# Two layer norms whose normalised copy is left out: x is turned and split block by block, and the row scale is applied at the eviction

## The chip, the cores and the metric

The kernel runs on one core of a Trainium2 chip. The metric is the device time of one execution in microseconds (us). Runs of one kernel mostly agree within 0.3%.

## The reference

Three layers over 256 tokens of width 2048, all in float32. The change touches the way into the first two, "ab" and "c". Both begin in the same way:

```python
def _rmsnorm(x, g):
    x32 = x.astype(jnp.float32)
    y = x32 * lax.rsqrt(jnp.mean(x32 * x32, axis=-1, keepdims=True) + NORM_EPS)
    return y * g.astype(jnp.float32)

h = jnp.matmul(_rmsnorm(x, norm_g).astype(x.dtype), w_in)      # 256 x 2048 by 2048 x 8192
# ab: 8 heads of a dilated mixture and 4 heads of differential attention, c: 16 heads of causal attention
x = x + jnp.matmul(y.astype(x.dtype), w_out)                   # 256 x 2048 by 2048 x 2048
```

The third layer (an ada-modulated mixer and a sparse expert layer) keeps its code.

## The kernel before

The tokens lie in two blocks of 128 partitions (T = 2). A GEMM is done in tiles of 512 output columns. Each tile is 16 steps (K = 16), one for each block of 128 rows of the weight. At each step ScalarE (ACT) rounds a 128x512 piece of the weight to `w_hi` (`split_hi_act`, L501, its instruction on L507), VectorE (DVE) writes the rest `w_lo` (`split_lo_dve`, L509), and TensorE (PE) runs six matmuls of 512 columns (`multiply_pe`, L514: hi by hi, hi by lo, lo by hi, for both token blocks). `w_hi` and `w_lo` are rings of four, so ACT can be at most four steps ahead of PE. SyncE (SP) streams the weight in pieces of two steps, 512 KB each, into `raw`, a ring of four pieces.

The other operand is x, normalised, turned (tokens along the free axis) and split in the same way into `xt_hi` and `xt_lo`. This was done in a stage of its own ahead of each of the two layers: `normalise_act` and `normalise_dve` (L425 to L432) take the mean square of each row, its root and a Newton step, and write the normalised copy `xn`. `turn_pe` (L434) then turns 32 blocks of 128x128 in eight groups, ACT and DVE apply the norm's weight g to them (L468, L488), and ACT and DVE split them (L473, L479). `end_of_stage` (L304) is a barrier of PE, ACT and DVE: each drains and waits for the other two. There is one behind the turning and one behind layer ab.

Inside a layer (`layer_act`, `layer_pe`, `layer_dve`, L615 to L702) the order of all work is written out by the step number s: 256 steps of the way in (16 tiles), then 64 steps of the way out (4 tiles). The attention of each pair of heads is placed at fixed steps between (`pairs_pe`, `pairs_act`, `pairs_dve`). `take_tile_act` (L635) evicts a tile of the way in from PSUM into `h` four steps into the next tile, `take_residual` (L706) adds a tile of the way out to x. GpSimd (POOL) streams 96 pieces of 1 MB of the ada weight into a ring of two (`ada_pool`, L528), and DVE adds each to an accumulator (`modulate`, L553) at the steps in ADA_SLOTS. The sum of such a piece over the partitions is `sum_cols_pe` (L970), at steps 38 and 42 of the way out.

At the start SP issues the load of x as one transfer, then sixteen constants, and then the weight (L2136 to L2146). PE's first instruction waits for all constants (L1849).

## Time and profile before

| | us |
|---|---|
| median of three runs | 3513.04 (3511.92 to 3519.26) |
| the profiled execution's own time | 3512.95 |
| its span in the trace | 3511.2 |

| engine | busy us | share |
|---|---|---|
| PE, matmuls | 3114.0 | 89% |
| DVE | 2489.3 | 71% |
| ACT | 1880.1 | 54% |
| POOL | 314.5 | 9% |

The span is the distance from the first to the last instruction in the trace; the rest of the execution's time, 1.75 us, lies around it. Times of single instructions below are from the span's start. A matmul's listed duration holds its way through the array, so that the pace is read from the distance between two starts. The granted clock is TensorE's, as a share of 2.4 GHz.

### The profile page before, as it was taken

The page shows a single profiled execution, that of the slowest core. Times are in us where ns is not written, and L with a number is a line of the kernel's source. Part 1 is how long each engine was busy: PE and PEld are TensorE (multiplying, and loading weights), DVE is VectorE, ACT ScalarE, POOL GpSimd, SP SyncE. Part 2 cuts the span into 40 slices and gives each one's busy share as a digit, 9 for nine tenths or more (in the row PEclk, how much of TensorE's full clock was granted, in tenths as well). Part 3 has the DMA queues.
Part 4 walks back from the last instruction along what each step waited for, and adds up shares of the span by engine and source line. Part 5 has one row for each costly group of instructions (what it writes and reads, how often), then busy time and mean ns, then how long its engine had stood idle before and what let it go on. Part 6 is the DMA issues. An engine that isn't in the chain of part 4 may idle for free. (4 is left out here: it accounts for less than half of the span.)

```text
span 3511.2 us, 45806 instructions
## 1 busy us (share of the span) xinstructions
PE 3114.0 (89%) x12426; PEld 2181.8 (62%) x12426; DVE 2489.3 (71%) x4415; ACT 1880.1 (54%) x4088; POOL 314.5 (9%) x422
## 2 busy tenths in 40 slices
PE   5999987999995959995795759999999899999997
PEld 4887766888884847884574612222222488888885
DVE  5778766777766857864655889998888655555555
ACT  4555544555544444544344447777777655555553
POOL 0000000000000000000000023333333100000000
PEclk9999998999997969996896955555555699999998
DMA  5666654666674907970053269999999755555553
GB/s 191 215 207 215 196 196 158 228 222 208 222 244 139 364 0 284 347 254 30 13 180 110 97 250 387 379 354 381 389 382 375 303 190 191 191 191 190 191 190 128
DMA packets 213960, 788.27 MB, mean 225 GB/s; under 512 B 18514, under 2 KB 19666, under 8 KB 151250
## 3 DMA queue, kind: packets, MB, share of 16 engines
q1 hardware_dynamic: 159904, 407.33, 34.1%
q0 software_dynamic: 50688, 369.12, 27.9%
q10 hardware_dynamic: 3252, 10.41, 0.8%
q8 instruction: 56, 0.92, 0.1%
q14 instruction: 60, 0.49, 0.0%
HBM read 781.55 MB, written 5.24 MB: 224 GB/s over the span
## 5 line engine op out<-in xcount | busy, mean ns | idle before, releaser
L511 DVE TENSOR_TENSOR w_lo<-raw,w_hi 128x512 fp32r<-128x512 f32 x880 | 584.8, 693 | 308.1 <-ACT w_hi L507 248.7
L507 ACT ACTIVATE w_hi<-raw 128x512 fp32r<-128x512 f32 x640 | 399.7, 631 | 497.4 <-PE bank L522 489.9
L1749 DVE CUSTOM_DVE_ANT_0 u_ring<-u_ring,bank 128x1024 f32<-128x1024 f32 x512 | 604.2, 1217 | 78.7 <-DMA u_ring<-in_peer_u,idx 54.7
L1816 DVE TENSOR_TENSOR w_lo<-v_raw,w_hi 128x512 fp32r<-128x512 f32 x512 | 354.1, 692 | 300.1 <-ACT w_hi L1800 300.1
L1661 PE MATMUL bank<-row_ring,three 3*128 3x512 bf16 x1024 | 511.1, 616 | 40.3 <-DVE act_in L1749 24.7
L1800 ACT ACTIVATE w_hi<-v_raw 128x512 fp32r<-128x512 f32 x512 | 323.5, 632 | 332.8 <-PE bank L1838 328.6
L520 PE MATMUL bank<-w_hi,xt_hi 128*128 128x512 f32 x1024 | 409.4, 400 | 19.9 <-DVE w_lo L511 19.9
L1836 PE MATMUL bank<-w_hi,vw_hi 128*128 128x512 f32 x1024 | 398.7, 389 | 7.2 <-DVE w_lo L1816 7.2
L1838 PE MATMUL bank<-w_hi,vw_lo 128*128 128x512 f32 x1024 | 404.4, 395 | 0.0
L1837 PE MATMUL bank<-w_lo,vw_hi 128*128 128x512 f32 x1024 | 402.5, 393 | 0.0
L522 PE MATMUL bank<-w_hi,xt_lo 128*128 128x512 f32 x1024 | 400.7, 391 | 0.0
L521 PE MATMUL bank<-w_lo,xt_hi 128*128 128x512 f32 x1024 | 400.5, 391 | 0.0
L558 DVE SCALAR_TENSOR_TENSOR acc<-ada_ring,c_col,acc 128x2048 f32<-128x2048 f32 x128 | 301.0, 2351 | 12.2 <-issue 0.4
L353 ACT ACTIVATE w_hi<-raw 128x512 fp32r<-128x512 f32 x304 | 190.3, 632 | 219.3 <-PE bank L372 188.4
L1632 POOL DMA_INDIRECT u_ring<-in_peer_u,idx x256 | 246.3, 962 | 456.2 <-DVE act_half L1749 452.9
L1661 PEld LDWEIGHTS bank<-row_ring,three 3*128 3x128 bf16 x1024 | 67.1, 106 | 316.8 <-DVE act_half L1749 223.0
L1669 PEld LDWEIGHTS bank<-hot_side,hot_side 128*128 128x128 f32 x512 | 128.1, 311 | 214.7 <-ACT hot_side L1712 208.0
L370 PE MATMUL bank<-w_hi,xt_hi 128*128 128x512 f32 x608 | 240.4, 395 | 18.2 <-DVE w_lo L511 15.0
L371 PE MATMUL bank<-w_lo,xt_hi 128*128 128x512 f32 x608 | 239.3, 394 | 0.0
L372 PE MATMUL bank<-w_hi,xt_lo 128*128 128x512 f32 x608 | 239.0, 393 | 0.0
L520 PEld LDWEIGHTS bank<-w_hi,xt_hi 128*128 128x128 f32 x1024 | 193.6, 189 | 61.0 <-issue 17.1
L1836 PEld LDWEIGHTS bank<-w_hi,vw_hi 128*128 128x128 f32 x1024 | 192.9, 188 | 50.6 <-issue 7.4
(336 smaller groups left out, 4564.1 us busy)
## 6 DMA issues: line engine op xcount, KB each, us to landing
v_raw<-in_peer_v SPq DMA_DIRECT2D x128, 1024.0 KB, 4.8
ada_ring<-in_ada_w POOLq DMA_DIRECT2D x96, 1024.0 KB, 5.6
raw<-in_w_in_ab SPq DMA_DIRECT2D x128, 512.0 KB, 3.9
raw<-in_w_in_c SPq DMA_DIRECT2D x128, 512.0 KB, 4.1
raw<-in_w_in SPq DMA_DIRECT2D x120, 512.0 KB, 6.0
raw<-in_w_out_ab SPq DMA_DIRECT2D x32, 512.0 KB, 4.5
raw<-in_w_out_c SPq DMA_DIRECT2D x32, 512.0 KB, 5.0
raw<-in_w_out SPq DMA_DIRECT2D x32, 512.0 KB, 4.4
```

Of the source, the lines that this page charges most:

```text
L507: act.activation(w_hi[:, s % WS, :], raw[:, q % RAW, s % KC, :], ACT.Copy).then_inc(hi_ready, 1)
L511: dve.tensor_tensor(w_lo[:, s % WS, :], raw[:, s // KC % RAW, s % KC, :], w_hi[:, s % WS, :].bitcast(F32), ALU.subtract).then_inc(raw_used, 1)
L520: pe.matmul(o, a_hi, b_hi, start=kk == 0, stop=False, skip_group_check=True)
L521: pe.matmul(o, a_hi, b_lo, start=False, stop=False, skip_group_check=True)
L522: last = pe.matmul(o, a_lo, b_hi, start=False, stop=kk == K - 1, skip_group_check=True)
L1661: last = pe.matmul(bank[:, 2 * hf + b, :], three[k:k + 3, :], rows_slot(j)[:, c:c + 512], start=True, stop=True)
L1749: dve.tensor_tensor_reduce(u, u, bank[:, 2 * hf:2 * hf + 2, :].rearrange("p b n -> p (b n)"), 1.0, 0.0, ALU.mult, ALU.add, (act_in, act_ha ...
L1800: act.activation(w_hi[:, c, :], v_raw[j][:, c * N:(c + 1) * N], ACT.Copy).then_inc(values_high, 1)
L1816: dve.tensor_tensor(w_lo[:, c, :], v_raw[j][:, c * N:(c + 1) * N], w_hi[:, c, :].bitcast(F32), ALU.subtract).then_inc(values_split, 1)
L1836: pe.matmul(o, a_hi, w_hi[:, c, :], start=first and j == 0, stop=False, skip_group_check=True)
L1837: pe.matmul(o, a_hi, w_lo[:, c, :], start=False, stop=False, skip_group_check=True)
L1838: last = pe.matmul(o, a_lo, w_hi[:, c, :], start=False, stop=True, skip_group_check=True)
```

## The change

- The normalised copy goes, with both normalise stages, both turning stages and the four barriers around them. x itself is turned, scaled by g and split, in eight pieces of two blocks (`x_turn_pe`, `x_high_act`, `x_low_dve`). The mean square's root r is applied to the rows of the tiles of the way in, as the scale operand of their eviction.
- Layer ab turns pieces 0 and 1 ahead of step 0 and pieces 2 to 7 at steps 0, 2, ... 10. PE waits ahead of each even step under 16 for `xt_lo` of that piece. Layer c has pieces 0 to 5 turned inside ab's way out (steps 38, 42, 46, 50, 55, 59) and pieces 6 and 7 at its own steps 6 and 8.
- The row sums of squares are taken at step 6 (ACT) and 7 (DVE) in ab, both on ACT at step 6 in c; the root and its Newton step at steps 10, 13 and 15.
- x is loaded in four pieces of 512 KB, each ahead of one piece of the weight on SP. eye and g of ab go to ACT's queue. Thirteen constants and c_col go to POOL's, behind x. ada's first two pieces come behind c_col.
- The accumulators are not cleared; the first addition writes. The first two slots of `modulate` in ab move from steps 4 and 18 to 20 and 23. The last residual tile of ab is added at step 3 of c. The lambda of ab moves by 14 to 22 steps.

```diff
+        LATE = (38, 42, 46, 50, 55, 59)
+        def x_turn_pe(pe, v, i):
+            if v:
+                pe.wait_ge(evacuated, PRE + plan["ab_out"]["t0"] + i // 2 + 1)
+            else:
+                pe.wait_ge(x_landed[i // 2], 16)
+            if i >= 2:
+                pe.wait_ge(lo_written, PRE + NG * v + i - 1)
+            for j in range(2):
+                for t in range(T):
+                    last = pe.transpose(bank[:, 4 + i % 2, (j * T + t) * P:(j * T + t + 1) * P],
+                                        x[:, t, (2 * i + j) * P:(2 * i + j + 1) * P], eye[:, :])
+            last.then_inc(blocks_turned, 1)
+        def x_high_act(act, v, i):
+            act.wait_ge(blocks_turned, PRE + NG * v + i + 1)
+            for j in range(2):
+                k = 2 * i + j
+                last = act.activation(xt_hi[:, k, :], bank[:, 4 + i % 2, j * S:(j + 1) * S], ACT.Copy, scale=(g_ab, g_c)[v][:, k:k + 1])
+            last.then_inc(hi_written, 1)
+        def x_low_dve(dve, v, i):
+            dve.wait_ge(hi_written, PRE + NG * v + i + 1)
+            for j in range(2):
+                k = 2 * i + j
+                last = dve.scalar_tensor_tensor(xt_lo[:, k, :], bank[:, 4 + i % 2, j * S:(j + 1) * S], (g_ab, g_c)[v][:, k:k + 1],
+                                                xt_hi[:, k, :].bitcast(F32), ALU.mult, ALU.subtract)
+            last.then_inc(lo_written, 1)
+        def layer_norm_pe(pe, v, s):
+            if v == 0 and s == 0:
+                pe.wait_ge(eye_landed, 32)
+                x_turn_pe(pe, 0, 0)
+                x_turn_pe(pe, 0, 1)
+            if v == 0 and s % 2 == 0 and s <= 10:
+                x_turn_pe(pe, 0, s // 2 + 2)
+            if v and s in (6, 8):
+                x_turn_pe(pe, 1, s // 2 + 3)
+            if s < K and s % 2 == 0:
+                pe.wait_ge(lo_written, PRE + NG * v + s // 2 + 1)
+        def layer_norm_act(act, v, s):
+            if v == 0 and s == 0:
+                act.wait_ge(eye_landed, 32)
+                x_high_act(act, 0, 0)
+            if v == 0 and s % 2 == 0 and s <= 12:
+                x_high_act(act, 0, s // 2 + 1)
+            if v and s in (0, 10, 12):
+                x_high_act(act, 1, {0: 5, 10: 6, 12: 7}[s])
+            if s == 6:
+                if v:
+                    act.wait_ge(evacuated, PRE + plan["ab_out"]["t0"] + 4)
+                    act.activation(h[:, 1, 6144:6144 + D], x[:, 1, :], ACT.Square, accum_out=small[:, 1:2])
+                else:
+                    for i in range(4):
+                        act.wait_ge(x_landed[i], 16)
+                act.activation(h[:, 0, 6144:6144 + D], x[:, 0, :], ACT.Square, accum_out=small[:, 0:1]).then_inc(act_step, 1)
+            if s == 13:
+                act.wait_ge(norm_step, PRE + 3 * v + 1)
+                act.activation(small[:, 4:4 + T], small[:, 2:2 + T], ACT.Sqrt).then_inc(act_step, 1)
+            if s == K + WS:
+                act.wait_ge(norm_step, PRE + 3 * v + 3)
+        def layer_norm_dve(dve, v, s):
+            if v == 0 and s == 0:
+                dve.wait_ge(eye_landed, 32)
+                x_low_dve(dve, 0, 0)
+            if v == 0 and s % 2 == 0 and s <= 12:
+                x_low_dve(dve, 0, s // 2 + 1)
+            if v and s in (1, 11, 13):
+                x_low_dve(dve, 1, {1: 5, 11: 6, 13: 7}[s])
+            if v == 0 and s == 7:
+                for i in range(4):
+                    dve.wait_ge(x_landed[i], 16)
+                dve.tensor_tensor_reduce(h[:, 1, 6144:6144 + D], x[:, 1, :], x[:, 1, :], 1.0, 0.0, ALU.mult, ALU.add, small[:, 1:2])
+                dve.drain()
+            if s == 10:
+                dve.wait_ge(act_step, PRE + 2 * v + 1)
+                dve.tensor_scalar(small[:, 2:2 + T], small[:, 0:T], 1.0 / D, EPS, ALU.mult, ALU.add).then_inc(norm_step, 1)
+            if s == 15:
+                dve.wait_ge(act_step, PRE + 2 * v + 2)
+                newton(dve, small[:, 6:6 + T], small[:, 4:4 + T], small[:, 2:2 + T], small[:, 62:62 + T])
+                dve.drain().then_inc(norm_step, 2)
...
+            pool.wait_ge(x_landed[3], 16)
+            pool.dma_start(c_col[:, :, :], A["c_cols"]).then_inc(c_landed, 16)
+            load(0, 0, 0)
+            load(1, 0, 1)
+            for dst, src in ((lam_in, "lam_ab"), (rope_cos, "rope_cos"), (rope_sin, "rope_sin"), (dil_neg, "dilated_neg"),
...
+            pool.wait_ge(const_landed, 16 * 13)
...
+                    if L["name"] == "ab" and n == 0 and q < 4:
+                        sp.dma_start(x[:, :, q * N:(q + 1) * N], A["x"][0].rearrange("(t p) d -> p t d", p=P)[:, :, q * N:(q + 1) * N]).then_inc(x_landed[q], 16)
...
+                if L["name"] == "ab" and s == 17:
+                    act.wait_ge(c_landed, 16)
+                    act.activation(c_col[:, :, :], c_col[:, :, :], ACT.Silu).then_inc(silu_done, 1)
+                    act.wait_ge(const_landed, 16 * 13)
...
+                if L["name"] == "ab" and s - 5 in LATE[:5]:
+                    x_high_act(act, 1, LATE.index(s - 5))
...
-                last = act.activation(h[:, t, at_:at_ + N], bank[:, 2 * (n % 2) + t, :], ACT.Silu if n % 4 == 0 else ACT.Copy)
+                last = act.activation(h[:, t, at_:at_ + N], bank[:, 2 * (n % 2) + t, :], ACT.Silu if n % 4 == 0 else ACT.Copy,
+                                      scale=small[:, 6 + t:7 + t])
...
+                if L["name"] == "ab" and s in LATE:
+                    x_turn_pe(pe, 1, LATE.index(s))
...
-            for i in range(2):
-                dve.memset(acc[i][:, :], 0.0)
             for s in range(256):
+                layer_norm_dve(dve, 0 if ab else 1, s)
+                if not ab and s == 3:
+                    take_residual(dve, plan["ab_out"], 3)
+                if ab and s == 16:
+                    dve.wait_ge(const_landed, 16 * 13)
...
+                if ab and s == 19:
+                    dve.wait_ge(silu_done, 1)
...
             layer_pe(pe, LAYER["ab"])
-            end_of_stage(pe, "pe")
-            turn_pe(pe, 1, xn, PRE + 6)
-            end_of_stage(pe, "pe")
             layer_pe(pe, LAYER["c"])
```

## Rows read from the trace of the kernel before

**Rows 1.** Busy time by stretch: engines with instruction counts, granted clock, DMA share, GB/s.
```profile
0.00:44.00 44.00, 8.61 (x33) 6.27 (x34) 20.12 (x33) 19.75 (x36) 1.46 (x6) 1.00 0.48 177
570.10:594.00 23.90, 6.12 (x34) 4.56 (x33) 19.02 (x31) 15.67 (x32) 0.00 (x0) 0.71 0.12 42
800.00:900.00 100.00, 99.11 (x471) 82.07 (x470) 76.15 (x129) 54.92 (x102) 2.11 (x4) 1.00 0.66 212
```
**Rows 2.** Timeline of the first 44 us: start, duration, engine, line, operation, idle before.
```profile
0.76 0.45 SPq L2136 DMA_DIRECT2D x<-in_x  x1
10.77 1.91 ACT L412 ACTIVATE xn<-x 128x2048 f32<-128x2048 f32 x1 [8.01 <-DMA x<-in_x]
20.22 0.16 DVE L2009 TENSOR_TENSOR lam<-lam_in 128x1 f32<-128x1 f32 x1 [15.86 <-DMA subln<-in_subln_ab]
20.61 2.29 DVE L417 CUSTOM_DVE_ANT_0 xn<-x 128x2048 f32<-128x2048 f32 x1 [0.17 <-issue]
23.43 0.17 DVE L400 RECIPROCAL small<-small 128x2 f32<-128x2 f32 x1 [0.27 <-ACT small L414]
24.68 1.29 DVE L427 TENSOR_SCALAR xn<-x,small 128x2048 f32<-128x2048 f32 x1
26.11 2.79 PE L448 MATMUL bank<-eye_sb,xn 128*128 128x128 f32 x12 [26.11 <-DVE xn L427]
```
**Rows 3.** Timeline of PE: the first steps of layer ab, and where tile 1 begins.
```profile
43.76 0.76 PE L520 MATMUL bank<-w_hi,xt_hi 128*128 128x512 f32 x1 [8.45 <-DVE w_lo L511]
47.69 0.39 PE L520 MATMUL bank<-w_hi,xt_hi 128*128 128x512 f32 x1
47.92 0.39 PE L521 MATMUL bank<-w_lo,xt_hi 128*128 128x512 f32 x1
67.66 0.39 PE L520 MATMUL bank<-w_hi,xt_hi 128*128 128x512 f32 x1
```
**Rows 4.** Timeline of PE between the two layers, and a turning in the stream.
```profile
117.98 1.03 PE L788 MATMUL bank<-eye_sb,h 128*128 128x128 f32 x8
118.77 0.47 PE L520 MATMUL bank<-w_hi,xt_hi 128*128 128x512 f32 x1
...
569.75 0.39 PE L522 MATMUL bank<-w_hi,h_r 128*128 128x512 f32 x1
594.00 0.76 PE L520 MATMUL bank<-w_hi,xt_hi 128*128 128x512 f32 x1 [8.12 <-DVE w_lo L511]
597.62 0.40 PE L520 MATMUL bank<-w_hi,xt_hi 128*128 128x512 f32 x1
```
**Rows 5.** Groups by line and shape, 0 to 1100 us: busy us, mean ns, idle before.
```profile
L507 ACT ACTIVATE w_hi<-raw 128x512 fp32r<-128x512 f32 x640 | 399.7, 631 | 497.4 <-PE bank L522 489.9 <-issue 3.5 <-DMA raw<-in_w_out_c 1.3
L511 DVE TENSOR_TENSOR w_lo<-raw,w_hi 128x512 fp32r<-128x512 f32 x640 | 427.9, 695 | 250.1 <-ACT w_hi L507 248.7
L468 ACT ACTIVATE xf<-bank,g_ab 128x128 f32<-128x128 f32 x16 | 4.9, 355 | 0.6 <-PE bank L448 0.6
L924 DVE SCALAR_TENSOR_TENSOR h<-bank,stat,h 128x256 f32<-128x256 f32 x8 | 3.5, 479 | 0.3
L558 DVE SCALAR_TENSOR_TENSOR acc<-ada_ring,c_col,acc 128x2048 f32<-128x2048 f32 x80 | 188.1, 2351 | 7.4
L710 DVE TENSOR_TENSOR x<-bank,x 128x512 f32<-128x512 f32 x16 | 10.3, 682 | 3.3 <-PE bank L522 3.3
```
**Rows 6.** A weight piece (KB, us to landing); then POOL's first issues, SP's slowest.
```profile
raw<-in_w_in_ab SPq DMA_DIRECT2D x21, 512.0 KB, 4.0
...
2.22 1.26 POOL L534 DMA_DIRECT2D ada_ring<-in_ada_w  x2 [1.76 <-DVEq L2005]
5.53 4.17 SPq L2142 DMA_DIRECT2D lam_in<-in_lam_ab  x1
```
**Rows 7.** Timeline of ACT at step 20 of layer c: a table load inside the stream.
```profile
618.23 1.28 ACT L641 ACT_TABLE_LOAD   x1
619.52 1.09 ACT L641 ACTIVATE h<-bank 128x512 f32<-128x512 f32 x2
```

More of the change, by code:

```diff
@@ L247, in bass_hybrid_stack_kernel @@
         bank = ctx.enter_context(nc.psum_tensor("bank", [P, 8, 512], F32))
-        x_landed, const_landed, aux_landed = sem("x_landed"), sem("const_landed"), sem("aux_landed")
+        x_landed = [sem(f"x_landed{i}") for i in range(4)]
+        eye_landed, c_landed, const_landed, aux_landed = (sem(n) for n in ("eye_landed", "c_landed", "const_landed", "aux_landed"))
         w_landed = [sem(f"w_landed{i}") for i in range(RAW)]
@@ L557, in modulate @@
             o = acc[to][:, :]
-            done = dve.scalar_tensor_tensor(o, ada_ring[:, i % 2, :], c_col[:, v, k:k + 1], o, ALU.mult, ALU.add)
+            if to < 2 and k == 0:
+                done = dve.tensor_scalar(o, ada_ring[:, i % 2, :], c_col[:, v, 0:1], None, ALU.mult)
+            else:
+                done = dve.scalar_tensor_tensor(o, ada_ring[:, i % 2, :], c_col[:, v, k:k + 1], o, ALU.mult, ALU.add)
             if last:
@@ L618, in layer_act @@
                 n, kk = s // K, s % K
+                layer_norm_act(act, 0 if L["name"] == "ab" else 1, s)
                 if n and kk == WS:
@@ L621, in layer_act @@
                 pairs_act(act, L, s)
-                if L["name"] == "ab" and s == 14:
+                if L["name"] == "ab" and s == 2:
+                    act.wait_ge(rows_cleared, 1)
+                    act.dma_start(acc[2][0:1, :], A["ada_b_rows"][:, 0, :]).then_inc(bias_row_landed, 16)
+                if L["name"] == "ab" and s == 17:
+                    act.wait_ge(c_landed, 16)
+                    act.activation(c_col[:, :, :], c_col[:, :, :], ACT.Silu).then_inc(silu_done, 1)
+                    act.wait_ge(const_landed, 16 * 13)
+                if L["name"] == "ab" and s == 32:
                     lam_act(act)
@@ L649, in layer_pe @@
                     pe.wait_ge(evacuated, PRE + g["t0"] + n - 1)
+                layer_norm_pe(pe, 0 if L["name"] == "ab" else 1, s)
                 pairs_pe(pe, L, s)
-                if L["name"] == "ab" and s == 8:
+                if L["name"] == "ab" and s == 24:
                     lam_pe(pe)
@@ L677, in layer_dve @@
             first = 0 if ab else 24
-            for i in range(2):
-                dve.memset(acc[i][:, :], 0.0)
             for s in range(256):
+                layer_norm_dve(dve, 0 if ab else 1, s)
[3 more added lines that the diff above has]
+                    dve.wait_ge(const_landed, 16 * 13)
+                    dve.tensor_tensor(lam[:, 0:1], lam_in[:, 0:1], lam_in[:, 1:2], ALU.mult)
+                    dve.tensor_tensor(lam[:, 1:2], lam_in[:, 2:3], lam_in[:, 3:4], ALU.mult)
+                    dve.drain().then_inc(aux_ready, 1)
+                if ab and s == 19:
+                    dve.wait_ge(silu_done, 1)
                 pairs_dve(dve, L, s)
                 split_lo_dve(dve, g, s)
-                if ab and s == 18:
+                if ab and s == 40:
                     lam_dve(dve)
-                if s % 64 in ADA_SLOTS:
-                    i = 8 * (s // 64) + ADA_SLOTS.index(s % 64)
+                slots = ADA_SLOTS_FIRST if ab and s < 64 else ADA_SLOTS
+                if s % 64 in slots:
+                    i = 8 * (s // 64) + slots.index(s % 64)
                     modulate(dve, first + i // 2, i % 2, i // 2, i % 2, i % 2 == 1)
@@ L690, in layer_dve @@
                 pairs_dve(dve, L, 256 + s)
+                if ab and s - 6 in LATE[:5]:
+                    x_low_dve(dve, 1, LATE.index(s - 6))
                 if s in (34, 36, 52):
@@ L701, in layer_dve @@
             dve.drain().then_inc(row_summed, 1)
-            take_residual(dve, g, 3)
+            if not ab:
+                take_residual(dve, g, 3)
+        ADA_SLOTS_FIRST = (20, 23, 28, 31, 34, 46, 49, 62)
         ADA_SLOTS = (4, 18, 28, 31, 34, 46, 49, 62)
@@ L1913, in act_program @@
                 act.sem_inc(s_, PRE)
-            act.wait_ge(x_landed, 16)
-            normalise_act(act, x, 0)
-            turn_act(act, 0, ((g_ab, None), 0))
-            act.wait_ge(const_landed, 16 * 16)
-            act.activation(c_col[:, :, :], c_col[:, :, :], ACT.Silu).then_inc(silu_done, 1)
-            end_of_stage(act, "act")
-            act.wait_ge(rows_cleared, 1)
-            act.dma_start(acc[2][0:1, :], A["ada_b_rows"][:, 0, :]).then_inc(bias_row_landed, 16)
+            act.dma_start(eye[:, :], A["eye"]).then_inc(eye_landed, 16)
+            act.dma_start(g_ab[:, :], A["norm_ab"]).then_inc(eye_landed, 16)
             layer_act(act, LAYER["ab"])
-            end_of_stage(act, "act")
-            normalise_act(act, x, 1)
-            turn_act(act, 1, ((g_c, None), NG))
-            end_of_stage(act, "act")
             layer_act(act, LAYER["c"])
@@ L2135, in _ @@
         def _(sp):
-            sp.dma_start(x[:, :, :], A["x"][0].rearrange("(t p) d -> p t d", p=P)).then_inc(x_landed, 16)
-            for dst, src in ((eye, "eye"), (rope_cos, "rope_cos"), (rope_sin, "rope_sin"), (dil_neg, "dilated_neg"),
-                             (dil_count, "dilated_count"), (cau_neg, "causal_neg"), (g_ab, "norm_ab"), (g_c, "norm_c"),
-                             (lam_in, "lam_ab"), (c_col, "c_cols"), (ada_bias, "ada_b_cols"), (g_mix, "norm_mix_2"),
-                             (g_ffn, "norm_ffn_2"), (wg, "w_gates")):
-                ap = dst[:, :, :] if len(dst.shape) == 3 else dst[:, :]
-                sp.dma_start(ap, A[src]).then_inc(const_landed, 16)
-            sp.dma_start(gate_b[:, :], A["b_gate_2"].partition_broadcast(P)).then_inc(const_landed, 16)
-            sp.dma_start(subln[:, :], A["subln_ab"].rearrange("a n -> (a n)").partition_broadcast(P)).then_inc(const_landed, 16)
             for name in ("ab", "c"):
```

38 lines of the change are left out of this document (14 added, 24 removed).

## The prediction
> **What bounds the kernel now.** I read the busy time of stretches first. In an undisturbed stretch of layer c, PE is busy 99.11 us of 100 at the full clock; ACT and DVE have 55 and 76 [rows 1]. So the layers are paced by PE, and anything that only ACT, DVE or a queue does beside it is free while it stays inside the lead that the rings give. The same view shows the exceptions: in the first 44.0 us PE does 8.6 us of work, and from 570.1 to 594.0 it does 6.1 [rows 1]. These are the stages that make and turn the normalised copy. The timeline of the first is a chain: x lands at 10.7; DVE is held until 20.2 by the last constant, because it computes lambda first; its sum of squares begins only at 20.61; the Newton step takes 23.43 to 24.68; the first turning comes at 26.11 [rows 2], and the first matmul of the GEMM at 43.76 [rows 3]. There is no transfer in the way in the second half: 0.12 DMA share in the gap between the layers [rows 1].
>
> PE's clock costs a little too. The first nine matmuls take 43.76 to 47.69, 0.437 us each, which is the 1.2 GHz level; behind 47.69 the distance is 0.227 (47.69 to 47.92), the 2.4 GHz level [rows 3]. PE had stood idle before. The granted clock listed for the first 44 us is 1.00 although this start is slow [rows 1], so that I go by the distances. A step is six matmuls, 1.36 us at the high level. Tile 1 begins at 67.5 (96 matmuls, 87 of them behind 47.69 at 0.227: 67.4; the row at 67.66 is the nearest first of three [rows 3]).
>
> **Part 1, the start of layer ab.** What remains ahead of the first matmul is: x piece 0, eye and g, turning, high, low, the split of the first weight piece.
> - The nearest row for a 512 KB transfer is a weight piece, 4.0 us from issue to landing [rows 6]; the far bound is x itself, 2 MB in 10.0 (0.76 to 10.77) [rows 2]. It is issued at 0.76, so it lands at 4.8. eye and g go by ACT's queue after the start-up of that engine; I take 5.6 for these, between 4.8 and 9. Pieces 1 to 3 follow with a weight piece between each; at 2 MB in 10 us, while POOL's 2 MB moved as well, two pieces are at most 2.6 to 5.0 apart, so piece 3 is there at about 13 to 18, and no turning is late by that: PE needs it at step 8.
> - Turning one piece is four transposes. In the cold stretch twelve took 2.79 [rows 2], 0.215 apart, so 0.86; in the stream eight took 117.98 to 118.77 [rows 4], so 0.4.
> - `x_high` is two ACTIVATEs of 128x256 from PSUM with a scale pointer. The trace has none; 128x128 takes 0.355 [rows 5] and 128x512 has a distance of 0.545 (1.09 for two) [rows 7]. I take 0.43 each, 0.86 for the piece, bounds 0.7 and 1.1. `x_low` is two of 128x256 on DVE; the nearest is L924 with 0.479 [rows 5]; half of a 128x512 split, 0.35, is the lower bound. 0.92 a piece.
> - Chain: 5.6, first turning and its way through the array 1.1, high of piece 0 0.86 (7.5), low of 0 and low of 1 1.84 (9.3), `w_lo` of step 0 0.70 [rows 5]. The GEMM begins at 10.1. Turning 2 is hidden in this. If every term is at its end: 8.5 to 14.
>
> Tile 0 then takes 16 steps, 21.8, plus 1.9 for the 1.2 GHz level ((0.437 - 0.227) x 9, one such start as before), plus five turnings in the stream, 3 to 7: 2.2 with one of them at the low level. What waits come on top:
> - The new chain from turning to multiplication. The piece that PE needs at step s+2 is turned at step s. From there: turning 0.65 to its last write, high 0.86, low 0.92, `w_lo` 0.70, four hand-overs of 0.06: 3.4. PE has 0.4 + 2 x 1.36 = 3.1 of work. That is 0 to 0.3 short each of six times, but at the low level PE has over 5, and the squares below leave room for ACT and DVE to catch up. 0.3 in all; bound 2.
> - ACT's square at step 6, 1.91 and its read-out 0.19, stands before `w_hi` of step 6, behind `x_high` of piece 4, which PE releases at step 4. The chain 0.65 + 0.86 + 2.1 + 0.63 + 0.70 + 0.2 = 5.1, against 3.1 to 3.6: 1.5 late.
> - DVE's at step 7, 2.29 and more [rows 2], before `w_lo` of step 7: 2.45 + 0.70 against 0.4 + 1.36: 1.4 to 1.8 late. Behind both waits `raw_used`, and so PE and the next weight piece; the ring of four pieces (8 steps) covers the transfer.
> - The root at step 13 (table load 1.28 [rows 7] and 0.2) before `w_hi`: 0.5. Newton at step 15 (1.25 [rows 2]) finds DVE with its lead again: 0.
> Together 4.1; bounds 1 and 8. Tile 1 begins at 10.1 + 21.8 + 1.9 + 2.2 + 4.1 = 40.1. The gain is 67.5 - 40.1 = 27.4, bounds 20 and 32.
>
> **Part 2, constants and ada.** Fourteen small loads, two of 1 MB with them, go to POOL behind x. POOL's issue took 0.63 each (1.26 for two) [rows 6], so 16 issues from 13 on end at 23; 2 MB of ada and 1.4 MB of constants move beside a weight stream that PE draws at 512 KB in 3.1 us. The transfer rate of x and ada together, 4 MB in 12, puts the last constant at 28 to 33. DVE wants it at step 16, which is ahead of PE at about 36: hidden by 3 to 8 us. If not, ACT at step 17, `w_hi` behind it, and PE wait one for one.
>
> **Part 3, between the layers.** The last matmul of ab starts at 569.75 and has its 0.23; the first of c starts at 594.00 [rows 4]: 24.0. The first nine take 594.00 to 597.62 [rows 4], 3.62 where 2.04 would do: 1.6 more. 25.6 goes, the two clearings of accumulators with it. Against it:
> - Eight turnings of 0.4: 3.2 on PE.
> - Inside ab's way out, five pieces of high (0.86) and low (0.92). ACT has some 0.7 idle each step (497.4 us over 640 steps [rows 5]) and DVE 0.39 (250.1 over 640): over 26 steps covered; where low falls beside a `modulate` of 2.35 or a residual of 1.3 [rows 5] it may be late. 1.0.
> - At c's step 3 the residual (2 x 0.68) and at 4 a `modulate` (2.35) [rows 5]: both wait for nothing but ab's last matmul, so from the start of PE's step 0 the residual 1.4, two `w_lo` 1.4, `modulate` 2.35 and `w_lo` of step 5 0.70 end at 5.9, due at 6.8. Covered.
> - At c's step 6 both squares on ACT, 4.2, behind `w_hi` of step 5, which needs step 1 multiplied: 2.7 + 0.63 + 4.2 + 0.63 + 0.70 + 0.2 = 9.1 after step 0 began, due 8.2: 0.9 late. Bounds 0 and 3.
> 25.6 - 3.2 - 1.0 - 0.9 = 20.5, bounds 15 and 22.5.
>
> **Part 4, costed at nothing.** The scale pointer in 64 evictions: ACT's idle hides up to 0.2 a tile; without it that is 6 us. The first ada piece as a multiplication only, earlier: DVE time that nobody waits for. The same work behind layer c runs unchanged, from its barriers on.
>
> Two rules of the Trainium skill speak against. Rows first: a table load inside the stream takes 1.28, and the eviction starts 0.01 behind it [rows 7]. "ScalarE: Activation LUTs", "What ACT_TABLE_LOAD costs", adds a drain of some 1.38 to every switch. By it the roots at step 13 would be later by up to 1.4 in each layer, and the sum 2.8 smaller; the row shows no such drain, and it has no part in the sum. The other is weighed with the second rival.
>
> **The sum.** 27.4 + 20.5 = 47.9. The profiled execution took 3512.95 (the median is 3513.04, so no correction): 3465.0. With the bounds of both parts, 35 to 54.5: 3458.5 to 3478.
>
> **Rivals.**
> - *The turned pieces pace the first tile.* If the hand-overs are longer, every even step under 16 waits, PE stays at 1.2 GHz through tile 0 and the squares add fully: 16 steps of 1.3 more in part is 8 to 10, and c's steps 6 to 15 another 5. 3480. For it: the chain of 3.4 against 3.1 is short already. Against: from step 7 DVE and ACT have room again, as 0.7 and 0.39 idle a step show.
> - *Late constants.* DVE's step 16 waits for thirteen transfers issued by POOL. If each costs more than 0.63 + its bytes, say 2.5 each, the last lands at 13 + 16 x 2.5 + 10 = 63, and 27 of the 48 are given back: 3492. For it: one of SP's small issues took 4.17 [rows 6]. Against: POOL's own two took 0.63. "SBUF — State Buffer" in the Trainium skill, "SBUF: two separate sides", says that GpSimd can't write a transfer's descriptors while DVE is in an operation that takes both port pairs; a 0.62 us issue became 3.1 in its measurement. By it the case is this one. No row here shows such an issue under a DVE operation of that kind.
> - *The same wait on the other side: slower than before.* Place: DVE ahead of `w_lo` of step 16. Price: PE stands from about 38 to the last constant. It decides when this lands after 38 + 48 = 86, that is when the fourteen small ones need over 4.2 each, as SP's lam_in did once (4.17). At 5.5 each, 13 + 77 + 10 = 100, it is 3527.
> - *No gain:* a barrier removed only moves the wait, since the layer is paced by DVE or the weight stream. Against: PE 99% busy in c [rows 1]. 3513.
>
> **How the numbers follow.** Forecast 0.75, own range 3458 to 3473. First rival 0.13 (3480), late constants 0.06 (3492), more gained than the bounds say 0.03 (3455), slower 0.02, none 0.01. The range of 3457 to 3480 takes in the forecast, its bounds and half of the first rival. Faster by over 0.2% (7 us, what a measurement of this kernel can tell): 0.97. Within: 0.01. Slower: 0.02.
>
> **What would show it.** In the changed trace the first matmul of 512 columns near 10 and that of tile 1 near 40; waits of PE for `w_lo` at steps 6 and 7 of 1 to 2 us; c's first matmul directly behind ab's last, without a start at the low level; c's step 6 late by about 1. DVE's lambda products (step 16) without a wait for a transfer. The prediction is wrong if PE waits for `xt_lo` or `w_lo` at each even step, if the first tile ends after 48, or if ab's way out grows by more than 5 us.

## The result and the profile after

| | before, us | changed, us |
|---|---|---|
| median (lowest to highest) | 3515.14 (3511.92 to 3519.26), 4 runs | 3479.40 (3471.52 to 3483.12), 4 runs |
| the profiled execution's own time | 3512.95 | 3471.52 |
| its span | 3511.2 | 3469.7 |

The ratio is 0.9891, 95% interval 0.9876 to 0.9906: faster. The two medians of the table are 35.7 us apart, those of a later repetition (0.9892, 0.9874 to 0.9910) 40.8. The forecast was 3465.0, range 3457 to 3480; between the two profiled executions 41.4 us went (41.5 by their spans) where 47.9 were forecast.

The view of stretches of the changed kernel (engines in the order PE, PE's weight loads, DVE, ACT, POOL, then granted clock, DMA share, GB/s), of the start and of the seam between the two layers:

```profile
0.00:44.00 44.00, 30.38 (x127) 23.57 (x128) 22.93 (x46) 22.65 (x42) 8.90 (x20) 1.00 0.76 262
546.00:570.00 24.00, 24.00 (x111) 19.65 (x110) 18.50 (x34) 15.92 (x27) 0.53 (x1) 1.00 0.72 224
```

PE is busy 30.4 us of the first 44, where it had 8.6 [rows 1]. The seam, in which it worked 6.1 of 24 us [rows 1], has no idle time left at all. (In such a timeline row, x8 is the number of instructions merged into it, and a bracket gives the idle time before it and what ended that.) The timeline of the start:

```profile
8.57 1.94 PE L515 MATMUL bank<-eye_sb,x 128*128 128x128 f32 x8 [8.57 <-DMA g_ab<-in_norm_ab]
9.74 1.28 ACT L523 ACT_TABLE_LOAD   x1 [9.74 <-PE bank L515]
11.04 1.56 ACT L523 ACTIVATE xt_hi<-bank,g_ab 128x256 fp32r<-128x256 f32 x4
14.39 0.76 PE L609 MATMUL bank<-w_hi,xt_hi 128*128 128x512 f32 x1 [0.30 <-DVE w_lo L600]
19.22 0.43 PE L611 MATMUL bank<-w_hi,xt_lo 128*128 128x512 f32 x1
24.07 1.92 ACT L561 ACTIVATE h<-x 128x2048 f32<-128x2048 f32 x1
27.24 2.29 DVE L579 CUSTOM_DVE_ANT_0 h<-x 128x2048 f32<-128x2048 f32 x1
27.46 0.47 PE L609 MATMUL bank<-w_hi,xt_hi 128*128 128x512 f32 x1 [0.95 <-DVE w_lo L600]
30.35 0.50 PE L609 MATMUL bank<-w_hi,xt_hi 128*128 128x512 f32 x1 [1.26 <-DVE w_lo L600]
42.60 0.15 DVE L804 TENSOR_TENSOR lam<-lam_in 128x1 f32<-128x1 f32 x1
44.24 0.39 PE L609 MATMUL bank<-w_hi,xt_hi 128*128 128x512 f32 x1
44.98 1.25 ACT L757 ACTIVATE h<-bank,small 128x512 f32<-128x512 f32 x2
```

The first turning waits for g_ab, not for x. Behind it stands a table load for which PE waits too. The GEMM begins at 14.39 (before: 43.76 [rows 3]) and tile 1 at 44.24. Before, tile 1 began at 67.66: the row that the prediction took for the nearest one [rows 3] is PE's 97th matmul of the GEMM, the first of tile 1. So 23.4 us are gained here. The two squares (24.07, 27.24) stand ahead of the two waits of PE (27.46, 30.35). Lambda at 42.60 has no bracket: the constants had landed. The view of transfers lists how long after its issue each landed (KB, us), of the first 50 us:

```profile
x<-in_x SPq DMA_DIRECT2D x4, 512.0 KB, 7.7
g_ab<-in_norm_ab ACTq DMA_DIRECT2D x1, 8.0 KB, 6.6
subln<-in_subln_ab POOLq DMA_DIRECT2D x1, 128.0 KB, 7.7
```

The 8 KB of g_ab took 6.6 us behind pieces of 512 KB that SP had issued at the same time. At the seam, first PE and then the squares on ACT and PE's turning at c's step 6:

```profile
549.94 0.39 PE L611 MATMUL bank<-w_hi,h_r 128*128 128x512 f32 x1
550.17 0.40 PE L609 MATMUL bank<-w_hi,xt_hi 128*128 128x512 f32 x1
```
```profile
553.66 1.90 ACT L557 ACTIVATE h<-x 128x2048 f32<-128x2048 f32 x1
555.55 1.90 ACT L561 ACTIVATE h<-x 128x2048 f32<-128x2048 f32 x1
558.37 0.60 PE L515 MATMUL bank<-eye_sb,x 128*128 128x128 f32 x4
```

The last matmul of ab and the first of c are 0.23 apart; before, they were 24.25 apart (569.75 and 594.00 [rows 4]).

A landmark behind everything that was changed is the first turning of heads in layer c, at its step 53. It stands here first as before, then in the changed kernel, then in the repetition of the changed kernel:

```profile
667.70 1.03 PE L788 MATMUL bank<-eye_sb,h 128*128 128x128 f32 x8
```
```profile
623.43 1.04 PE L921 MATMUL bank<-eye_sb,h 128*128 128x128 f32 x8
```
```profile
623.48 1.04 PE L921 MATMUL bank<-eye_sb,h 128*128 128x128 f32 x8
```

44.3 us are gained up to there: 23.4 by tile 1 of ab, and 20.9 from there on. The 20.9 are a sum. Between tile 1 and ab's last matmul 3.6 are given back (the gain there is 569.75 - 549.94 = 19.8), since six turnings now lie in ab's way out; the four of them in its steps 44 to 63 add 2.0 us, 0.50 each. Between the two layers 24.0 are gained, and 0.4 from c's first matmul to the landmark. At the end of layer c (first sum over the partitions, 1086.32 and 1043.66) 42.7 are left, at the end of the span 41.5.

### The profile page after: what moved, and what is told of

Read it like the earlier page. It is cut to its first block and busy times, and to the rows that moved or that the text cites. A ratio compares the mean times of both kernels' runs of the same rounds, so it can differ in the third digit from the quotient of the medians.

```text
span 3469.7 us, 45761 instructions
## 1 busy us (share of the span) xinstructions
PE 3109.5 (90%) x12426; PEld 2175.4 (63%) x12426; DVE 2466.7 (71%) x4407; ACT 1871.2 (54%) x4070; POOL 321.9 (9%) x436
## 3 DMA queue, kind: packets, MB, share of 16 engines
q10 hardware_dynamic: 3540, 10.48, 0.8%
## 5 line engine op out<-in xcount | busy, mean ns | idle before, releaser
L1794 PE MATMUL bank<-row_ring,three 3*128 3x512 bf16 x1024 | 510.6, 616 | 44.3 <-DVE act_in L1882 28.5
L662 DVE SCALAR_TENSOR_TENSOR acc<-ada_ring,c_col,acc 128x2048 f32<-128x2048 f32 x122 | 286.9, 2352 | 12.4 <-issue 1.4
```

The lines of the kernel that those rows point to most:

```text
L1794: last = pe.matmul(bank[:, 2 * hf + b, :], three[k:k + 3, :], rows_slot(j)[:, c:c + 512], start=True, stop=True)
```

## The experiments

In all of them "c's turning" is that landmark.

**1. The changed kernel again.** No edit.

> The changed kernel as it is. Its first four executions spread from 3471.5 to 3483.1 us, the profiled one being the fastest, while its trace ends 41.5 us before that of the kernel before. Theory A: the gain in the layers is 44 us in every execution (first turning of c's first pair of heads 44.3 earlier), and the spread comes from stages behind layer c. Then this trace too has that turning at 623 to 625, and the median over more executions comes to 38 to 42 less than before. Theory B: the wait at the start or between the layers differs from execution to execution; then the turning at c's step 53 lies 5 to 10 us later in a slow execution.

3479.39 (3473.50 to 3488.61, 6 runs). c's turning is at 623.48, c's end at 1043.67, 0.05 and 0.01 from the first trace, but the span is 3476.8 instead of 3469.7. So at these two marks the traces repeat to 0.05 us, and all of the 7 us between the two executions arises behind layer c. It builds up there step by step: the same instruction of PE is 5.5 later at 1712, 6.2 at 1877 and 7.1 at 2746. Inside layer ab the two traces don't repeat as well: they are within 0.1 us of each other up to step 240, then up to 2.9 apart (at step 272), and together again at step 298. From c's end to the end of the span, eight of the thirteen traces of this study have 2424.8 to 2426.9 us (those of the kernel before and of the changed kernel among them) and five have 2431.5 to 2433.7 (this one 2433.1). Why there are two groups I have not found; the landmark is the sharper measure of this change. The executions of the kernel before spread by 19 us beside this run (3510.62 to 3529.84), so that a median of four to six can be some us off.

**2. Layer ab alone.** Layer c is normalised and turned in a stage of its own, as before; the accumulators are not cleared.

```diff
-                if L["name"] == "ab" and s in LATE:
-                    x_turn_pe(pe, 1, LATE.index(s))
...
+            end_of_stage(pe, "pe")
+            turn_pe(pe, 1, xn, PRE + 6)
+            end_of_stage(pe, "pe")
```

> Only layer ab has the change; c is normalised and turned in its own stage between barriers, as before. If the two parts add (theory A): tile 1 of ab begins at 44.2, the gap between the layers is 24 us again with a start at the low clock level, c's step 53 comes 21 us later than in the changed kernel (644.4), time 23 us under before. If instead a part of ab's gain is given back when c's stage comes (theory B, its DVE or transfers were behind anyway), the gain is 15 or less.

3492.19 (3487.04 to 3496.88), ratio 0.9927 (0.9907 to 0.9947). c's turning is at 640.18: 27.5 of the 44.3 are there, where 23.3 were expected. They are 24.8 at tile 1 of ab, less 1.0 on the way to ab's last matmul, 3.6 between the layers and 0.1 behind. The start came out 1.4 better than in the changed kernel (tile 1 at 42.81): the first matmul is at 14.06, and six matmuls from there run at the 1.2 GHz level instead of eleven. The distance between ab's last and c's first matmul is 20.7 (545.91 and 566.60) instead of 24.25. Before, the last thing ahead of c's first matmul were the two clearings of the accumulators, and they are gone here too; they stood at

```profile
589.40 1.76 DVE L679 MEMSET acc<- 128x2048 f32 x1 [0.59 <-DVEq L307]
591.54 1.76 DVE L679 MEMSET acc<- 128x2048 f32 x1 [0.38 <-issue]
```

3.8 us of DVE (589.40 to its `w_lo` at 593.22), of which 3.6 show in the distance. The stage in front of c itself is the other 20.5 of it (20.7 less the 0.23 of the changed kernel); net of the turnings in ab's way out and of the difference at the start, 16.7 of them arrive at the landmark.

**3. Layer c turns at its own steps**, pieces 0 and 1 ahead of step 0 and 2 to 7 at steps 0 to 10, as ab does, instead of inside ab's way out.

```diff
-            if v and s in (6, 8):
-                x_turn_pe(pe, 1, s // 2 + 3)
+            if v and s == 0:
+                pe.wait_ge(evacuated, PRE + plan["ab_out"]["t0"] + 3)
+                x_turn_pe(pe, 1, 0)
+                x_turn_pe(pe, 1, 1)
+            if v and s % 2 == 0 and s <= 10:
+                x_turn_pe(pe, 1, s // 2 + 2)
```

> Layer c turns all eight pieces in its own first steps, as ab does, instead of six of them inside ab's way out. Theory A (the turning in the way out is free but for PE's 0.4 us a piece): the same PE work, but c's step 0 now waits for turning, high, low and w_lo: 3 to 5 us more before c's step 2, and the squares at step 6 hit ACT together with the pieces: 1 to 3 more. Time 4 to 7 us over the changed kernel, c's step 53 at 627.5 to 630.5. Theory B (the two steps from turning to use set the pace): each even step waits, 10 us or more.

3483.42 (3480.18 to 3485.18), ratio 0.9895 (0.9876 to 0.9914); c's turning at 633.60, 10.1 later than in the changed kernel, where 4 to 7 were expected. The timeline of PE, at the seam and at c's step 6:

```profile
550.45 1.03 PE L515 MATMUL bank<-eye_sb,x 128*128 128x128 f32 x8
552.98 0.63 PE L515 MATMUL bank<-eye_sb,x 128*128 128x128 f32 x4 [1.50 <-DVE xt_lo L530]
554.36 0.47 PE L617 MATMUL bank<-w_hi,xt_hi 128*128 128x512 f32 x1 [0.76 <-DVE w_lo L608]
567.01 0.47 PE L617 MATMUL bank<-w_hi,xt_hi 128*128 128x512 f32 x1 [2.73 <-DVE w_lo L608]
567.58 0.63 PE L619 MATMUL bank<-w_hi,xt_lo 128*128 128x512 f32 x1
570.57 0.56 PE L617 MATMUL bank<-w_hi,xt_hi 128*128 128x512 f32 x1
```

The start of c costs 3.9 (550.45 to 554.36), and c's first tile 28.9 instead of 22.9 (next tile at 583.28, against 573.10). In it the two squares cost a wait of 2.73, since neither ACT nor DVE has any lead when they come, and behind that wait PE runs at the 1.2 GHz level for seven more matmuls (0.43 apart from 567.58 to 570.57); the four more turnings in the tile come on top. Not all of the 10.1 belongs to the placement. This kernel leaves out the six turnings in ab's way out, 3.0 us at 0.50 each, and yet ab's last matmul is at 550.22, 0.3 later than the changed kernel's: some 3.3 were lost inside ab, where both kernels are the same but for these turnings, in the way that experiments 9 to 11 look at. The start of c and its first tile cost 9.9 more, and the turnings that are not in the way out give 3.0 back: 6.9 for the placement, at the upper end of what was expected. The medians are 4 us apart, the landmarks 10.1; the scatter behind layer c (experiment 1) is large enough for that, but whether it is the cause isn't shown.

**4. g_ab and eye first, the table load early.**

```diff
-            act.dma_start(eye[:, :], A["eye"]).then_inc(eye_landed, 16)
-            act.dma_start(g_ab[:, :], A["norm_ab"]).then_inc(eye_landed, 16)
+            act.wait_ge(rows_cleared, 1)
+            act.activation(small[:, 60:61], ones[:, 0:1], ACT.Copy)
...
+            sp.dma_start(g_ab[:, :], A["norm_ab"]).then_inc(eye_landed, 16)
+            sp.dma_start(eye[:, :], A["eye"]).then_inc(eye_landed, 16)
```

> g and eye are issued first on SP's queue, ahead of x, instead of on ACT's, and ACT does one tiny operation early so that its table load lies there. In the changed kernel g landed at 8.5 us behind the packets of x and the weight, PE's first transpose came at 8.57, and the table load stood from 9.74 to 11.02 before the first high half: first matmul of the GEMM at 14.39. Theory A (the small transfer and the table load are what the forecast missed): first transpose at 5.5 to 6.5, first matmul at 10.3 to 11.5, tile 1 at 40.5 to 41.5, 3 to 4 us gained. Theory B (x's or the weight's piece is what ends last): the first matmul stays at 12.5 or later, since they now come 1 us later.

3468.53 (3463.11 to 3475.57), ratio 0.9860 (0.9838 to 0.9881). The timeline of its start:

```profile
1.48 1.28 ACT L2042 ACT_TABLE_LOAD   x1 [1.48 <-PEq L2284]
5.94 1.94 PE L515 MATMUL bank<-eye_sb,x 128*128 128x128 f32 x8 [5.94 <-DMA x<-in_x]
9.29 1.12 PE L515 MATMUL bank<-eye_sb,x 128*128 128x128 f32 x4 [1.41 <-DMA x<-in_x]
10.48 0.77 PE L609 MATMUL bank<-w_hi,xt_hi 128*128 128x512 f32 x1
13.09 0.39 PE L609 MATMUL bank<-w_hi,xt_hi 128*128 128x512 f32 x1
```

Now x is what the first turning waits for, and the GEMM begins at 10.48, 3.9 earlier. The low-level stretch is shorter too: six matmuls (10.48 to 13.09) instead of eleven (14.39 to 19.22). Tile 1 begins 5.1 earlier (39.18), and c's turning is at 616.99, 6.4 earlier.

**5. The order of the queues alone, on the kernel before.** eye and g_ab get a semaphore of their own and go out right behind x; lambda is computed behind the turning. Copy, stage and barriers stay.

```diff
-            pe.wait_ge(const_landed, 16 * 16)
+            pe.wait_ge(eye_landed, 32)
...
+            sp.dma_start(eye[:, :], A["eye"]).then_inc(eye_landed, 16)
+            sp.dma_start(g_ab[:, :], A["norm_ab"]).then_inc(eye_landed, 16)
```

> The kernel before with one thing changed: g and eye come right behind x and have their own semaphore, and lambda, which needs the last constant, is computed behind the turning instead of ahead of the sum of squares. The normalised copy and all barriers stay. Theory A (in the first 44 us before, 9.8 us were DVE held by the constants): sum of squares at 10.9 instead of 20.6, first matmul of the GEMM at 34 instead of 43.8, 9 to 10 us gained; so of the 23.3 that the change gained up to tile 1, some 10 came from the order of the transfers and 13 from leaving the copy out. Theory B (the turning needs something else that lands as late): under 4.

3505.96 (3503.32 to 3509.75), ratio 0.9958 (0.9942 to 0.9973). Two rows of its timeline:

```profile
10.33 2.29 DVE L417 CUSTOM_DVE_ANT_0 xn<-x 128x2048 f32<-128x2048 f32 x1 [5.96 <-DMA x<-in_x]
34.19 0.77 PE L520 MATMUL bank<-w_hi,xt_hi 128*128 128x512 f32 x1 [8.45 <-DVE w_lo L511]
```

DVE's sum of squares starts 10.3 earlier and the GEMM 9.6 earlier than before (43.76 [rows 3]). So of the 29.4 us by which the changed kernel's GEMM begins earlier, 9.6 need no algebra at all: they were DVE and PE waiting for constants that they didn't need yet. The other 19.8 are not the copy and the stage alone. The two clearings of the accumulators stand on the path here too, between the last turned block and the first `w_lo`; in this kernel the first of them is

```profile
29.60 1.76 DVE L679 MEMSET acc<- 128x2048 f32 x1 [1.24 <-ACTq L307]
```

and `w_lo` comes at 33.42, 3.8 later. That leaves 16.0 for the copy, the turning in one piece and the barriers together. But c's turning is at 661.57, only 6.1 earlier: 3.4 were lost on the way, with no new wait. That led to experiments 9 to 11.

**6. No sums of squares.** It leaves out the squares of both layers, in place of which the sums are set to one.

```diff
-                act.activation(h[:, 0, 6144:6144 + D], x[:, 0, :], ACT.Square, accum_out=small[:, 0:1]).then_inc(act_step, 1)
+                act.sem_inc(act_step, 1)
...
-                dve.tensor_tensor_reduce(h[:, 1, 6144:6144 + D], x[:, 1, :], x[:, 1, :], 1.0, 0.0, ALU.mult, ALU.add, small[:, 1:2])
-                dve.drain()
```

> The changed kernel without the sums of squares of both layers (three of the four operations on ACT, one on DVE; a constant stands for the sums), all semaphores as before. Theory A: PE's waits at ab's steps 6 and 7 (1.2 and 1.4 us) and the quarter of a us at c's step 6 go, tile 1 begins at 41.4 to 41.8 instead of 44.2, c's first turning of heads at 620.3 to 621. Theory B (the turned pieces pace the first tile anyway): the waits move to the next steps, under 1 us gained.

3476.23 (3471.36 to 3479.09), ratio 0.9867 (0.9843 to 0.9891). The summary of PE's waits in tile 0 (line, releaser, us in total, times, longest), first of the changed kernel, then of this one:

```profile
PE bank L609 <- DVE w_lo L600: 2.5, 3, 1.3
```
```profile
PE bank L606 <- DVE w_lo L597: 0.3, 1, 0.3
```

The 0.3 that is left is the wait ahead of the first matmul of all (14.16; in the changed kernel 0.30 at 14.39), so that inside tile 0 the squares' 2.2 us were the only waits. Without the squares tile 0 is evicted 3.36 earlier (41.62 against 44.98), more than the 2.2, since its first matmul is also 0.2 earlier and two fewer matmuls run at the low level. The expectation at c's turning failed all the same: it is at 623.45, where it was. The evictions of ab's tiles keep the 3.4 us up to 291, have 2.1 of it left at 353, and none at 575.

**7. Constants late.** POOL issues the thirteen only when DVE is behind step 8.

```diff
+            pool.wait_ge(raw_used, RAW * KC + 9)
```

> The changed kernel with the thirteen constants issued only when DVE has done step 8 (about 31.7 us instead of 16.2). In the changed kernel the last of them landed at 30.2, and DVE asks for them at 42.6: 12 us of cover. Theory A: now they land at 45 to 46.5, DVE's step 16 waits 2.5 to 4 for them and PE 1.5 to 3.5; c's first turning of heads at 625 to 627 instead of 623.4. So the price is one for one once the cover is used up. Theory B (issues from POOL are slowed by DVE's operations in this stretch): they land after 50, 5 us or more.

3479.55 (3463.19 to 3481.51), ratio 0.9865 (0.9833 to 0.9898). Three rows of its timeline:

```profile
31.66 0.54 POOL L633 DMA_DIRECT2D lam_in<-in_lam_ab  x1 [15.55 <-DVE w_lo L600]
43.68 0.16 DVE L805 TENSOR_TENSOR lam<-lam_in 128x1 f32<-128x1 f32 x1 [1.31 <-DMA subln<-in_subln_ab]
44.87 0.47 PE L609 MATMUL bank<-w_hi,xt_hi 128*128 128x512 f32 x1 [0.79 <-DVE w_lo L600]
```

Issued 15.5 us later, the constants make DVE wait 1.31 and PE 0.79, less than the 2.5 to 4 and the 1.5 to 3.5 that were expected, because the last had landed by 43.7 and not at 45 or later. Tile 1 begins at 44.87, 0.6 later than in the changed kernel. c's turning comes at 625.96, 2.5 later, inside the expected range, but by luck: the other 1.9 arise later in ab, where no constant is waited for. The wait of the second rival exists at the place it named; the changed kernel has about 12 us of slack before it (landing at 30.2, wanted at 42.6).

**8. Best of both.** Experiment 4 with ab's squares in quarters of 512 columns at steps 5, 7, 9 and 11, the root at 14, Newton at 17.

```diff
+            if v == 0 and s in (5, 7, 9, 11):
+                i = (s - 5) // 2
+                act.wait_ge(x_landed[i], 16)
+                last = act.activation(h[:, 0, 6144 + i * N:6144 + (i + 1) * N], x[:, 0, i * N:(i + 1) * N], ACT.Square,
+                                      accum_out=small[:, 16 + i:17 + i])
```

> start_first, and ab's sums of squares cut in quarters of 512 columns at steps 5, 7, 9 and 11, where neither engine has a turned piece to split; the root follows at step 14 and Newton at 17. Theory A (the two waits come from one operation longer than the lead of the ring): the waits of 0.95 and 1.27 go or shrink under 0.3, tile 1 about 2 us earlier, c's first turning of heads at 614.5 to 615.5 instead of 617.0. Some 50 us under the kernel before. Theory B: the read-outs and fixed parts of eight operations eat it; no change.

3467.34 (3463.87 to 3472.30), ratio 0.9851 (0.9828 to 0.9874), span 3462.0, c's turning at 615.67. The quarters (0.63 on ACT, 0.69 on DVE) take the waits at steps 6 and 7 away; the one wait left is the 0.3 ahead of the first matmul. Tile 1 begins 2.0 earlier than in experiment 4 (37.15 against 39.18), and 1.3 of it arrive at the landmark. Of all kernels run this one has the lowest median, though its interval overlaps with that of experiment 4.

**9 to 11. A shift at the start, nothing else.** One, two or four ACTIVATEs of 128x512 ahead of the first `x_high`, where PE waits for it. One execution each.

```diff
+                for i in range(4):
+                    act.activation(h[:, 0, 6144 + i * N:6144 + (i + 1) * N], bank[:, 4, 0:N], ACT.Copy)
                 x_high_act(act, 0, 0)
```

> The changed kernel with one more ACTIVATE of 128x512 on ScalarE ahead of the first x_high, in a stretch in which PE waits for it. It moves the first matmul of the GEMM by the 0.5 to 0.6 us of one such eviction, from 14.39 to about 14.9, and nothing else. Theory A (a shift at the start is not kept, because the clock behind each stop of PE in layer ab depends on when the stop falls): tile 1 begins 0.5 to 0.6 later, but the first turning of the heads in layer c, at 623.43 and 623.48 in the two traces of the unshifted kernel, moves by something else, between -2 and +3 us. Rival B (a shift is carried through, and what the kernel without the squares lost is due to the squares): c's turning moves by 0.5 to 0.6, to 624.0.

> Two such ACTIVATEs: the first matmul at about 15.5. Theory A: layer c's turning anywhere between 621.5 and 626.5, and the deviation from 1.1 arises behind stops of PE in the attention of layer ab, where the low-level stretch has another length. Rival B: 624.6.

> Four such ACTIVATEs: the first matmul at about 16.6. Theory A: layer c's turning between 622.5 and 627.5, not on a line with the other two shifts. Rival B: 625.7.

| ACTIVATEs | first matmul | eviction of tile 1 | c's turning |
|---|---|---|---|
| 0 | 14.39 | 66.98 | 623.43 |
| 1 | 14.62 | 67.00 | 624.27 |
| 2 | 15.78 | 68.42 | 624.84 |
| 4 | 16.05 | 68.25 | 628.64 |

The shifts came out smaller than expected since g_ab landed at other times (8.3 to 9.0), but they do what they were for. With one ACTIVATE, layer ab is in step with the changed kernel to 0.02 at tile 1's eviction and 0.84 later at c's turning. With four it is 1.27 later at tile 1 and 5.2 later at c. The waits are the same: between 44 and 623 the longest group, DVE's `prob`, holds PE for 10.6 us in four waits in the changed kernel and for 10.7 in these. What differs is the clock behind the same waits. At the first of them, the kernel before, the changed one and the one with four ACTIVATEs show:

```profile
338.71 0.55 PE L866 MATMUL bank<-eye_sb,prob 128*128 128x128 f32 x3 [2.32 <-DVE prob L852]
339.56 0.39 PE L522 MATMUL bank<-w_hi,xt_lo 128*128 128x512 f32 x1
339.79 0.39 PE L520 MATMUL bank<-w_hi,xt_hi 128*128 128x512 f32 x1
```
```profile
315.63 0.55 PE L999 MATMUL bank<-eye_sb,prob 128*128 128x128 f32 x3 [2.32 <-DVE prob L985]
316.64 0.63 PE L611 MATMUL bank<-w_hi,xt_lo 128*128 128x512 f32 x1
317.07 0.63 PE L609 MATMUL bank<-w_hi,xt_hi 128*128 128x512 f32 x1
319.63 0.41 PE L609 MATMUL bank<-w_hi,xt_hi 128*128 128x512 f32 x1
```
```profile
317.12 0.90 PE L1002 MATMUL bank<-eye_sb,prob 128*128 128x128 f32 x3 [2.33 <-DVE prob L988]
318.25 0.63 PE L613 MATMUL bank<-w_lo,xt_hi 128*128 128x512 f32 x1
320.38 0.45 PE L612 MATMUL bank<-w_hi,xt_hi 128*128 128x512 f32 x1
```

The stop is 2.32 or 2.33 us long each time. Behind it the matmuls are 0.227 apart (2.4 GHz) before the change; 0.43 apart (1.2 GHz) up to 319.63 after it; and with four ACTIVATEs the three transposes are already slow (0.90 for 0.55), but the stretch ends sooner. Rival B, a constant shift, falls with the kernel of four ACTIVATEs: 1.27 at tile 1 became 5.2. Theory A is right in that a shift isn't carried through, but its reason, that the clock depends on when the stop falls, isn't shown, and one execution of each kernel can't show it. The two executions of the changed kernel itself speak against it in its simple form. They reach the next such stop 0.05 us apart, the changed kernel's first trace above, its repetition below:

```profile
425.99 0.55 PE L999 MATMUL bank<-eye_sb,prob 128*128 128x128 f32 x3 [2.33 <-DVE prob L985]
427.07 0.39 PE L609 MATMUL bank<-w_hi,xt_hi 128*128 128x512 f32 x1
```
```profile
426.04 0.90 PE L999 MATMUL bank<-eye_sb,prob 128*128 128x128 f32 x3 [2.33 <-DVE prob L985]
428.02 0.63 PE L609 MATMUL bank<-w_hi,xt_hi 128*128 128x512 f32 x1
```

The same fourth matmul behind the stop comes 0.95 later in the repetition, whose matmuls are 0.43 apart up to 428.88, where the first trace has 0.23 from the second on. So part of what moves inside ab differs between executions of one kernel, although these two agree to 0.05 at the landmark. How much of the shifts here, and of the losses in experiments 3 and 5 to 7, is of this kind, one trace of each doesn't show. What decides how the clock answers to a stop stays open.

## Why the prediction was right, and where it missed

The sign, the mechanism, the places of the waits and the seam were right, and the start of the GEMM was 4.3 too early; the profiled time was 6.5 us above the forecast: 4.0 up to tile 1, 2.8 given back behind the landmark, less 0.4 between the two. The median, 3479.4, is another 7.9 above, and that it lies within the range is luck: it is beyond the 3478 to which the bounds of the sum reach, and only 0.6 inside the 3480 that was put there for the first rival, which didn't come. The profiled executions before and after are both of the group with 2425 to 2427 us behind layer c (experiment 1), so that they compare like with like. By the steps:

| step | forecast | measured |
|---|---|---|
| first turning | 5.6 | 8.57, for g_ab (issued at 1.89, 6.6 to landing) |
| from there to the GEMM | 4.5 | 5.82, a table load of 1.28 among it |
| GEMM begins | 10.1 | 14.39 |
| tile 0 | 30.0 | 29.85 |
| its waits | 4.1 | 2.2 |
| gain at tile 1 | 27.4 | 23.4 |
| from tile 1 to ab's last matmul (six turnings 2.4, late pieces 1.0) | -3.4 | -3.6 |
| between the two layers | 24.0 | 24.0 |
| from c's first matmul to the landmark (low level 1.6, two turnings 0.8, squares 0.9) | -0.1 | 0.4 |
| the last three together | 20.5 | 20.9 |
| given back behind | 0 | 1.6 in layer c, 1.2 behind it |

- **The start chain was too short by 4.3**, two terms of it. I took a price for eye and g that had no row ("I take 5.6 for these, between 4.8 and 9"); the near end was wrong and the bound right. And the first ACTIVATE of the kernel needs its table: before, this load lay in the wait for x, where it costs nothing, and moving the first ACTIVATE onto the path put it there. The step that failed is "high of piece 0 0.86 (7.5)", which put the table load of 1.28 ahead of it at nothing. Experiment 4 takes both away, and the GEMM begins at 10.48 against the forecast 10.1: the rest of the chain was right: there the first piece of x landed 4.2 after its issue (forecast 4.0), and from the first turning to the GEMM it took 4.54 (forecast 4.5).
- **Tile 0 came out at 29.85 against 30.0, partly by errors that cancel.** Waits for the squares came where they were said, 0.95 and 1.26 by the bracket, 2.2 in all against 4.1; the low level lasted eleven matmuls instead of nine: (19.22 - 14.39) - 11 x 0.227 = 2.3, against 1.9. The remaining 1.4 or so lies in the turnings and around the waits; I did not split it. The pieces themselves: high 0.82 to 0.84, low 0.87 to 0.88, forecast 0.86 and 0.92. The 67.5 from which the gain was counted was 0.16 low (tile 1 began at 67.66).
- **The first rival did not come**: there is no wait at every even step. The 0.3 us by which the hand-over chain was said to be short shows as no wait of PE; I take it to be covered by ACT's and DVE's lead.
- **The late constants did not come**: POOL's thirteen issues were 0.53 apart, and lambda had 12 us to spare. Experiment 7 confirms the place of the wait; of DVE's 1.31 there PE paid 0.79, so that the price was below one for one. (In the rival "slower than before" the limit of 4.2 a transfer should be 4.5: 86 - 13 - 10 = 63 us for fourteen.) "SBUF — State Buffer" in the Trainium skill, "SBUF: two separate sides", would have made these issues some 3 us each under certain DVE operations; the longest of POOL's single issues here is 0.71, beside DVE's splits, so no such case shows in this kernel.
- **The seam** is right to 0.5 us in each term, as the table shows. Of its 24.0, experiment 2 gives 3.6 to the clearings and the rest to the stage; experiment 3 prices the place of the turnings at some 6.9. c's step 6 was forecast 0.9 late and waits 0.25.
- **The table load without a drain**: the row at 9.74 ends at 11.02, and the ACTIVATE starts at 11.04. "ScalarE: Activation LUTs" in the Trainium skill, "What ACT_TABLE_LOAD costs", would have it 1.38 later; as in [rows 7] the trace has no such gap.
- **Not in the sum at all** was that time gained early need not arrive. From the landmark to the end of layer c it was 1.6 us here, but the experiments show it as large as 3.4 up to the landmark, in both the kernel without squares and that with the order alone, and of either sign: the early start gained 3.9 at the first matmul and 6.4 at c. The 7 us between two executions of one kernel arise behind c; whether the clock makes these as well isn't shown.

## What to carry to other kernels

Removing a stage in front of a GEMM is worth nearly its whole length when PE is the bound behind it: 24.0 us here, less 3.6 for what moved into the layer ahead. It matters where the moved work is put: with the turnings at c's own steps 9.9 us came back at c's start, 3.0 of which were saved in the way out. Put the small operands of the first instruction ahead of the large ones in one queue, and give ScalarE its table while it has nothing to do: 8 KB in the wrong place and one table load cost 3.9 us. A third of the gain at the first matmul (9.6 of 29.4) was a wait for constants that nobody needed yet, and another 3.8 the clearing of accumulators, so look at what stands on the path and at a wait's semaphore before changing the algebra. Gains of 1 to 4 us ahead of a long stretch with stops of TensorE have to be measured at a landmark right behind the edit, and are not to be counted on at the end.

## What the hardware showed unexpectedly

- The same stop of PE, 2.32 us, is followed by no low-level matmul or by a stretch of 2 to 3 us at 1.2 GHz (five to seven matmuls 0.43 apart). Two executions of one kernel differ in this at a stop that they reach 0.05 us apart. The summary by stretch hides some of this: it gives a granted clock of 1.00 for the first 44 us of the changed kernel, in which eleven matmuls are 0.43 apart; the distances between starts are the safer reading.
- A transfer of 8 KB took 6.6 us from issue to landing on ACT's queue beside SP's pieces of 512 KB; issued first on SP, it took 1.8, and both g_ab and eye had landed when x did, at 5.94.
- Two executions of the same kernel agree to 0.01 us after 1043 us of work, although they were up to 2.9 apart on the way, and differ by 7 at the end.
